# The recurrence's block inverses by Newton steps in four groups over eight PSUM banks, instead of squarings in two halves over four

## The reference

```python
def step(state, inp):
    r_t, w_t, k_t, v_t, kk_t, a_t = inp
    sa = jnp.einsum('bhvk,bhk->bhv', state, -kk_t)
    state = (state * w_t[:, :, None, :]
             + sa[..., :, None] * (kk_t * a_t)[..., None, :]
             + v_t[..., :, None] * k_t[..., None, :])
    out = jnp.einsum('bhvk,bhk->bhv', state, r_t)
    return state, out
...
o = jnp.zeros((B, S, H, N), f32)
for d in range(2):
    o = o + wkv7_scan(rh, heads(decay), kd, vh, kk, heads(a), reverse=(d == 1))
```

## Time and profile before

| | |
|---|---|
| median of three runs | 3305.81 us (3300.61, 3305.81, 3305.88) |
| the profiled execution's own time | 3306.75 us |
| its span, first to last instruction | 3305.0 us |
| TensorE busy | 3113.0 us, 94% of the span |
| VectorE busy | 2296.5 us, 69% |
| ScalarE busy | 975.3 us, 30% |
| GpSimd busy | 1106.5 us, 33% |
| the recurrence stage | 177 to 456.4 us of the span |

### The profile page before, as it was taken

The page is one execution under the profiler, slowest core; times in us unless marked ns, Lnnn a source line. Parts: engine busy times, 40 slices in busy tenths (PEclk is TensorE's granted clock), DMA queues, the critical chain, the costliest instruction groups (busy, mean ns, idle before and its releaser), DMA issues. The chain is left out here.

```text
span 3305.0 us, 57848 instructions
## 1 busy us (share of the span) xinstructions
PE 3113.0 (94%) x21263; PEld 2736.6 (83%) x21263; DVE 2296.5 (69%) x3997; ACT 975.3 (30%) x1689; POOL 1106.5 (33%) x766
## 2 busy tenths in 40 slices
PE   8979979999999999989999999889998999799989
PEld 6568857789999999989999987667886777578867
DVE  7677666779889898778888876576773326567731
ACT  2333431233433433333333332541120013311200
POOL 4231114222222122143333334124554332345543
PEclk9989999999999999999999999999999999899999
DMA  4000012257777877889999943022323220123323
GB/s 159 26 2 3 3 33 96 102 181 245 267 258 240 282 250 254 296 311 369 338 356 337 353 170 105 17 71 87 97 79 87 82 62 29 56 93 100 99 66 96
DMA packets 214343, 509.06 MB, mean 154 GB/s; under 512 B 18534, under 2 KB 102646, under 8 KB 210588
## 3 DMA queue, kind: packets, MB, share of 16 engines
q1 hardware_dynamic: 155420, 322.15, 29.1%
q0 software_dynamic: 36864, 134.23, 12.2%
q10 hardware_dynamic: 21888, 50.34, 4.0%
HBM read 454.21 MB, written 52.44 MB: 153 GB/s over the span
## 5 line engine op out<-in xcount | busy, mean ns | idle before, releaser
L188 PE MATMUL ev_acc<-ev_w_high,ev_high 128*128 128x384 f32 x1024 | 343.2, 335 | 9.3 <-DVE ev_w_low L2569 9.3
L190 PE MATMUL ev_acc<-ev_w_high,ev_low 128*128 128x384 f32 x1024 | 343.0, 335 | 0.0
L189 PE MATMUL ev_acc<-ev_w_low,ev_high 128*128 128x384 f32 x1024 | 343.0, 335 | 0.0
L2519 POOL DMA_INDIRECT ev_rows<-in_v,ev_list x128 | 179.3, 1401 | 328.0 <-DVE ev_row_sum L2574 305.1
L188 PE MATMUL up_ps<-ffn_high,up_high 128*128 128x512 f32 x704 | 276.8, 393 | 5.5 <-DVEq L667 5.5
L190 PE MATMUL up_ps<-ffn_high,up_low 128*128 128x512 f32 x704 | 275.6, 391 | 0.0
L189 PE MATMUL up_ps<-ffn_low,up_high 128*128 128x512 f32 x704 | 275.4, 391 | 0.0
L183 POOL TENSOR_TENSOR up_low<-normed,up_high 128x1024 fp32r<-128x1024 f32 x88 | 211.4, 2403 | 178.0 <-DVE up_high L178 178.0
L188 PE MATMUL eu_ps<-norm_unit_high,eu_high 128*128 128x384 f32 x768 | 265.5, 346 | 0.0
L190 PE MATMUL eu_ps<-norm_unit_high,eu_low 128*128 128x384 f32 x768 | 257.6, 335 | 0.0
L189 PE MATMUL eu_ps<-norm_unit_low,eu_high 128*128 128x384 f32 x768 | 257.3, 335 | 0.0
(11 more groups left out here) (642 smaller groups left out, 8133.4 us busy)
## 6 DMA issues: line engine op xcount, KB each, us to landing
normed<-in_u SPq DMA_DIRECT2D x128, 512.0 KB, 5.1
mixed<-in_v SPq DMA_DIRECT2D x128, 512.0 KB, 5.5
normed<-in_w_up SPq DMA_DIRECT2D x88, 512.0 KB, 3.5
expert_act<-mixed ACTq DMA_DIRECT2D x128, 192.0 KB, 4.2
expert_gates<-eu_gates ACTq DMA_DIRECT2D x24, 1024.0 KB, 6.8
expert_scores<-expert_gates SPq DMA_DIRECT2D x16, 1536.0 KB, 11.6
ev_act<-expert_act SPq DMA_DIRECT2D x128, 192.0 KB, 5.7
in_w_raw<-in_w_in SPq DMA_DIRECT2D x20, 512.0 KB, 3.5
```

Of the source, the lines that this page charges most:

```text
L188: nc.tensor.matmul(out, w_high.bitcast(F32R), x_high.bitcast(F32R), start=start, stop=False)
L189: nc.tensor.matmul(out, w_high.bitcast(F32R), x_low.bitcast(F32R), start=False, stop=False)
L190: return nc.tensor.matmul(out, w_low.bitcast(F32R), x_high.bitcast(F32R), start=False, stop=stop)
L2519: nc.gpsimd.indirect_dma_start(rows[:, b % 4, :], None, v, bass.IndirectOffsetOnAxis(ap=list_[:, b % 8:b % 8 + 1], axis=0)).then_inc(fetch ...
```

## The change

- The inverse X of A = I - L is found by Newton's steps, X becomes 2X - XAX. For each of levels 1 to 5 TensorE forms "E" from X and L - I, ScalarE copies it, TensorE forms "T" from E and X, and VectorE does X = 2X + T in one `scalar_tensor_tensor`. The squarings are gone.
- The eight units go in four groups of two: an E and a T of a group are four products each, a copy or an update is 128x128 elements. E uses banks 3, 4, 5, 1 and T banks 0, 6, 7, 2.
- "Lt" and "L" are formed in blocks of 64: 16 products of 64x64x64 for Lt instead of 8 of 64x128x128, 24 for L instead of 8. VectorE copies each in two pieces of 128x256, with the masks for a 64 block made once ahead of the stage by six small copies. The off-diagonal block of L is copied by ScalarE ("low0", "low1").
- I + L transposed ("Tt") and L - I ("less") are made by GpSimd, after its part of `prepare`.
- The inverse has a tile of its own, and VectorE copies "sa0" ahead of "z_t".

The core of the diff, in this order: tiles and banks, GpSimd, ScalarE, VectorE, TensorE.

```diff
-        inverse_t = c.y[:, 9, :].rearrange("p (u s) -> p u s", s=HEAD)
+        inverse_t = sb("inverse_t", [P, 2 * ST, HEAD])
+        upper, lower, unit = (sb(x, [P, HEAD]) for x in ("block_upper", "block_lower", "block_unit"))
...
-        ab_bank, t_bank = (ps[3], ps[1]), (ps[0], ps[2])
+        e_bank, t_bank = (ps[3], ps[4], ps[5], ps[1]), (ps[0], ps[6], ps[7], ps[2])
+        c_bank, y_bank = (ps[3], ps[1]), (ps[0], ps[2])
+        of_group = lambda i: slice(2 * i, 2 * i + 2)
...
+                def front(d, m):
+                    units_ = unit[:, :].unsqueeze(1).to_broadcast([P, 2 * ST, HEAD])
+                    dve_s[d].wait(pool, m, "Lt1")
...
+                    pool_s[d].ends(nc.gpsimd.tensor_tensor(inverse_t[:, :, :], square[:, :, HEAD:P], units_, ALU.add), "Tt")
+                    dve_s[d].wait(pool, m, "L1")
...
+                    pool_s[d].ends(nc.gpsimd.tensor_tensor(pw[:, :, 0:HEAD], pw[:, :, 0:HEAD], units_, ALU.subtract), "less")
...
+                    if at == 2:
+                        dve_s[d].wait(act, m, "L1")
+                        for h in range(2):
+                            act_s[d].ends(nc.scalar.activation(pw[second_half[d], ST * h:ST * h + ST, HEAD:P], ps[2 + h][second_half[d], :, HEAD:P], ACT.Copy), f"low{h}")
...
+                    for n in range(1, LEVELS):
+                        for i in range(4):
+                            pe_s[d].wait(act, m, f"E{n}{i}")
+                            act_s[d].ends(nc.scalar.activation(square[:, of_group(i), 0:HEAD], e_bank[i][:, 0:2, 0:HEAD], ACT.Copy), f"E{n}{i}")
+                            if i % 2:
+                                beside((n - 1, i // 2))
...
+                    beside((0, 1))
+                    for n in range(1, LEVELS):
+                        for i in range(4):
+                            mine = inverse_t[:, of_group(i), :]
+                            pe_s[d].wait(dve, m, f"T{n}{i}")
+                            done.ends(nc.vector.scalar_tensor_tensor(out=mine, in0=mine, scalar=2.0, in1=t_bank[i][:, 0:2, 0:HEAD], op0=ALU.mult, op1=ALU.add), f"T{n}{i}")
+                            if i % 2:
+                                beside((n, i // 2))
...
-                    pe_s[d].wait(dve, m, "z_t")
-                    done.ends(nc.vector.tensor_copy(z_t[:, :, :], ps[4][:, :, :]), "z_t")
...
                         if n == 0:
+                            done.wait(dve, m, "X1")
                             done.ends(nc.vector.tensor_copy(s_a, u), "sa0")
+                            pe_s[d].wait(dve, m, "z_t")
+                            done.ends(nc.vector.tensor_copy(z_t[:, :, :], ps[4][:, :, :]), "z_t")
...
+                        if kind in ("Lt", "L"):
+                            for x in half:
+                                for h in range(2):
+                                    ins = nc.tensor.matmul(ps[2 * n + h][x, t, 0:HEAD], to_[half[h], x], of_[half[h], x], start=True, stop=True)
+                        if kind == "L":
+                            for h in range(2):
+                                ins = nc.tensor.matmul(ps[2 * n + h][second_half[d], t, HEAD:P], to_[half[h], second_half[d]], of_[half[h], first_half[d]], start=True, stop=True)
...
+                    for n in range(1, LEVELS):
+                        for i in range(4):
+                            if n == 1:
+                                pool_s[d].wait(pe, m, "less")
+                                if i == 3:
+                                    dve_s[d].wait(pe, m, "qk1")
                             else:
+                                dve_s[d].wait(pe, m, f"T{n - 1}{i}")
+                            for k in range(2):
+                                u = 2 * i + k
+                                for x in half:
+                                    ins = nc.tensor.matmul(e_bank[i][x, k, 0:HEAD], inverse_t[x, u, :], pw[x, u, 0:HEAD], start=True, stop=True)
+                            pe_s[d].ends(ins, f"E{n}{i}")
+                        for i in range(4):
+                            act_s[d].wait(pe, m, f"E{n}{i}")
+                            if n == 1 and i == 0:
+                                dve_s[d].wait(pe, m, "qk0")
+                            if n == 1 and i == 3:
+                                act_s[d].wait(pe, m, "U")
+                            for k in range(2):
+                                u = 2 * i + k
+                                for x in half:
+                                    ins = nc.tensor.matmul(t_bank[i][x, k, 0:HEAD], square[x, u, 0:HEAD], inverse_t[x, u, :], start=True, stop=True)
+                            pe_s[d].ends(ins, f"T{n}{i}")
```

More of the change, by code:

```diff
@@ L1265, in _ @@
                         prepare(d, m)
+                        front(d, m)
             @block.scalar
@@ L1331, in _ @@
                     prepare(0, 0, at)
-                for at in ("begin", 0, "end"):
+                for at in ("begin", 0, 2, "end"):
                     front(0, 0, at)
@@ L1371, in prepare @@
                         done.ends(nc.vector.tensor_tensor(f[d][:, here], flat(chunks(gt)[:, here, last]), mid[:, there], ALU.add), "f")
-                def mask_of(d, kind):
-                    first, other, with_self = (c.upper, c.lower, c.upper_eq) if d == 0 else (c.lower, c.upper, c.lower_eq)
-                    return {"Lt": first, "L": other, "zk": first, "qb": with_self, "qk": with_self}[kind]
                 def front(d, m, at):
@@ L1381, in front @@
                     kind, done = kinds[at], dve_s[d]
-                    if kind == "qk":
-                        done.wait(dve, m, "Lt11")
-                        for x in range(2):
-                            unit = c.ident[half[x], half[x]].unsqueeze(1).to_broadcast([HEAD, 2 * ST, HEAD])
-                            done.ends(nc.vector.tensor_tensor(inverse_t[half[x], :, :], square[half[x], :, HEAD:P], unit, ALU.add), f"Tt{x}")
                     pe_s[d].wait(dve, m, kind)
-                    if kind == "Lt":
+                    if kind in ("Lt", "L"):
+                        block = mask_of(d, kind).to_broadcast([P, ST, HEAD])
@@ L1389, in front @@
                         for h in range(2):
-                            for x in range(2):
-                                block = mask_of(d, kind)[half[x], half[x]].unsqueeze(1).to_broadcast([HEAD, ST, HEAD])
-                                done.ends(nc.vector.tensor_tensor(square[half[x], ST * h:ST * h + ST, HEAD:P], ps[h][half[x], :, half[x]], block, ALU.mult), f"Lt{h}{x}")
+                            own = square[:, ST * h:ST * h + ST, HEAD:P] if kind == "Lt" else pw[:, ST * h:ST * h + ST, 0:HEAD]
@@ L1393, in front @@
+                            done.ends(nc.vector.tensor_tensor(own, ps[2 * at + h][:, :, 0:HEAD], block, ALU.mult), f"{kind}{h}")
                         return
                     for h in range(2):
-                        mask = mask_of(d, kind)[:, :].unsqueeze(1).to_broadcast([P, 4, P])
-                        dve_s[d].ends(nc.vector.tensor_tensor(to[d][kind][:, 4 * h:4 * h + 4, :], ps[2 * (at % 2) + h][:, :, :], mask, ALU.mult), f"{kind}{h}")
+                        done.ends(nc.vector.tensor_tensor(to[d][kind][:, ST * h:ST * h + ST, :], ps[2 * (at % 2) + h][:, :, :],
+                                                          mask_of(d, kind).to_broadcast([P, ST, P]), ALU.mult), f"{kind}{h}")
@@ L1398, in solve @@
                 def solve(d, m, beside):
                     done = dve_s[d]
-                    for n in range(LEVELS):
-                        for h in range(2):
-                            if n:
-                                mine = inverse_t[:, ST * h:ST * h + ST, :]
-                                pe_s[d].wait(dve, m, f"T{n}{h}")
-                                done.ends(nc.vector.tensor_tensor(mine, t_bank[h][:, :, 0:HEAD], mine, ALU.add), f"T{n}{h}")
-                            beside((n, h))
+                    beside((0, 1))
@@ L1485, in matrices @@
                         act_s[d].wait(pe, m, "vn")
+                    elif n == 2:
+                        dve_s[d].wait(pe, m, "Lt1")
+                    elif n == 3:
+                        dve_s[d].wait(pe, m, "L1")
+                        act_s[d].wait(pe, m, "low1")
                     else:
-                        dve_s[d].wait(pe, m, last_of[kinds[n - 2]])
+                        dve_s[d].wait(pe, m, "zk1")
                     for t in range(ST):
-                        for h in range(2):
-                            rows = slice(h * HEAD, (h + 1) * HEAD)
-                            ins = nc.tensor.matmul(ps[2 * (n % 2) + h][:, t, :], chunk(left, t)[rows, :], chunk(right, t)[rows, :], start=True, stop=True)
+                        to_, of_ = chunk(left, t), chunk(right, t)
+                        if kind in ("Lt", "L"):
+                            for x in half:
[4 more added lines that the diff above has]
```

(4 more changed lines are left out.)

76 lines of the change are left out of this document (25 added, 51 removed).

## The result

The kernel after the change takes 3270.93 us (median of four runs, 3267.22 to 3274.78), the kernel before it 3303.21 (four runs, 3297.81 to 3305.88): a ratio of 0.9905, with a 95% interval from 0.9893 to 0.9918. That is 32.3 us, between 27.1 and 35.3. Predicted were 3285 us and a gain of 21.

What follows compares the result with a forecast made beforehand. TensorE's weight loads were taken to bound the solves, the state chain and VectorE in turns the steps; 14.9 + 5.95 + 0.5 - 0.36 = 21.0 us off 3306.75, adjusted to the median, gave 3285, range 3275 to 3299 (likeliest case 3277 to 3292).

Steps and rivals of the forecast that it cites:

- What bounds the stage: Recurrence stage, 279.4 us: TensorE bounds the solves; what the stage saves should reach the program's end one for one.
- The undisturbed solve: Solve with nothing beside it: 320 loads, levels of 1.87 us set by TensorE, 9.53 us in all.
- The solve with `prepare`: Solves with `prepare` between: lumps add 2.90 or 2.21 us, giving 12.43 or 11.74; eight solves gain 14.9 us.
- E22: Level 2 of a solve: an E product group starts 1.42 us late (0.73 for direction 0) behind VectorE's differences.
- T32: Level 3 of a solve: a T product group is 0.45 us late behind ScalarE's exponential of 512 columns.
- E50: Start of a solve's level 5: TensorE idles, 0.93 us late, after z and f on VectorE delay level 4's updates.
- The steps: Steps stretches between solves: 0.57 us from sa0's new place, 0.94 in all before E; 5.95 us over seven, 0.5 for the last.
- The start: First front, standing alone: 0.24 us back, mask copies ahead of the first cumulative sum cost 0.6; net 0.36 lost.
- Small copies do not overlap: Rival for the solves: each further 128-wide copy adds 0.284 us, 4.8 in all, 3290; chance with dearer lumps 0.19.
- The update costs 0.42: Rival for the solves: VectorE's update takes 0.42 us, costing 17 us of the 21, time 3302; chance 0.10.
- The waits cost TensorE its pace: Rival for the solves: 0.18 us lost at each of 40 groups, 57.6 us in all, 3342; chance 0.07.
- Better: Rival: lumps fall where a group is late anyway, and a shorter restart (0.05): 3276; chance 0.06.

Runs made afterwards that it cites:

- The kernels with `prepare` spread: Changed kernel with each piece of `prepare` alone at a level's end: 3262.88 us, ratio 0.9867; with the mask copies also later, 3261.74 us.
- The bursts: Changed kernel plus six bursts of 16 unused 64x64x64 products, differing in the array quadrants that follow each other: whole execution 3282.90 us.
- the order over two quadrants: Changed kernel with Lt and L's diagonal blocks formed first on the two diagonal quadrants, then on the other two: 3278.89 us, ratio 0.992.

## Why the prediction was wrong

**What bounds the stage: right.** What was saved in the stage reached the end, 30.0 us by the traces and 32.3 (27.1 to 35.3) by the medians. The two profiled executions differ by 39.5 us (3306.75 and 3267.22), so 9.5 of these lie outside the stage, where the code is the same. The windows view puts 5.7 of them in one place: the same 1001 multiplications took 217.21 us from 2735.22 on before, at a mean granted clock of 0.92, and 211.49 us from 2701.38 on after, at 0.96. So most of it is the clock of these two executions and not the change. The 14 us by which the time lies below the forecast are then the 9.0 of the stage, 2.3 outside it, and 2.6 because the kernel before had a median of 3303.21 us in this set and 3305.81 when the forecast was made.

**The undisturbed solve: right.** 9.53 us predicted, 9.47 measured. A level is 1.87 us: TensorE sets the pace, and the copies come back in time.

**The solve with `prepare`: places right, prices each a little high.** In the first solve E22 1.31 us (predicted 1.42), T32 0.34 (0.45), E50 0.85 (0.93), f's exponential nothing (0.1), the end 0.15 (0.2). The common part is the restart: TensorE loads 0.05 us after the update it waits for (199.53 + 0.48 is the second update's end; the first ends near 199.81, the load is at 199.86), and the 0.11 was read from one row. Four solves at 11.96 for 12.43 and three at 11.25 for 11.74 make 3.3 of the 3.5 us missed here.

One of those prices was right by luck. The 1.92 us of z and f was read as work, though f has three columns. The timeline of the kernel before shows it beside GpSimd:

```profile
207.77 1.59 POOL L1260 TENSOR_TENSOR scan_ek<-mix_kd,scan_ek 128x512 f32<-128x512 f32 x1
...
208.17 1.22 DVE L1371 TENSOR_TENSOR scan_f<-mix_p,scan_mid 128x3 f32<-128x3 f32 x1
```

GpSimd's product ends at 209.36 and f at 209.39. In the kernel after the pair ends alike, 205.90 and 205.93. It was a wait for GpSimd, which no step of the prediction named. The kernels with `prepare` spread show that most of it can be avoided: f takes 0.37 us there on the mean.

**The steps: the step that failed.** The prediction said that L "follows 2.14 later as before", and that L takes "48 loads, 1.39 us for 0.97: 0.42 more on TensorE". Measured, L follows Lt by 1.67 us, and the next load follows L by 1.08 for the 1.48 predicted: 0.87 us a stretch less, which over seven is 6.1 of the 9.0 us by which the stage was missed. The 0.029 us a load was taken from the solve, whose products alternate between two quadrants; Lt and L go round four, at 0.015. The bursts and the order over two quadrants show 0.57 of the 0.87. The other 0.30 stays even over two quadrants. Of it 0.19 is counting: Lt in blocks of 64 was given the time of the wide products it replaced (1.10 us to the next load), though by the prediction's own 0.029 its 32 loads cost 0.93, and over two quadrants they took 0.91. The 0.11 that are left are L's (1.37 for 1.48), and no run takes them apart. All else in this part holds: `kv0` loads 0.44 us after z_t's copy began (predicted 0.44), Lt starts 2.39 after it (2.38), the rest of the stretch is 7.03 (7.0), and "less" hides.

**The start: mis-sized.** Six mask copies were put at 0.6 us between nothing and 1.38. They cost 1.45: the cumulative sum behind them begins 2.30 us after the table load for 0.85. Each is about 0.2 us long, though it has a quarter of the elements of the 0.23 us copy. With them the start lost 1.0 us for 0.36, and the granted clock had a share in it that no run parts: it stood at 0.50 for 14.7 us after the table load for 11.7 before.

**The rivals.** *Small copies do not overlap* did not come: levels are 1.87 us. With it falls the rule of the Trainium skill ("VectorE: DVE Perf Modes", the section on the TRN2 errata) as one that would decide here. It speaks for instructions of 512 elements and more; here updates twice as wide in half as many groups made a level 2.37 us for 1.87 and the stage 12.85 longer. *The update costs 0.42* fell: 284 ns over 160. *The waits cost TensorE its pace* fell: 9.41 us of loads in 9.47 with forty groups. *Better* came nearest, with its short restart of 0.05 right, and at 3276 was still 5 us too slow, since it looked for more in the solves alone and for nothing in the steps.

## What to carry to other kernels

Before a rate per load is carried from one place to another, look at which 64x64 quadrants of the array the successive products use: going round four gave twice the pace of two and four times that of one, for the price of a loop order. That is for 64 columns moving; with 128 the cut into four quadrants brought 0.1 us a stretch. In a loop that lives on a round trip, put side work on the returning engines one piece at a time at a level's end, and keep VectorE's operations on SBUF inputs away from GpSimd's products. A three-column operation of 1.2 us was a wait and not work.

## What the runs showed of the hardware

- fp32 64x64x64 products: 0.058 us a load on one quadrant, 0.029 on any two, 0.015 on four, at the full granted clock, whether or not the quadrants share rows or columns.
- VectorE and GpSimd hold each other up on SBUF. A VectorE operation on two SBUF inputs that began while a GpSimd product ran ended a fixed time after the product, whatever was left of it: 0.55 us after for the difference of 128x512 (1.65 us long for 0.68), 0.02 us after for the 128x3 of f (1.22, 0.30 or 0.18 us long). Copies of 64x64 from SBUF to SBUF did the same, 0.05 us after (two in 1.45 us for 0.41). GpSimd's product went from 1.27 to 1.59 us beside z. The Trainium skill ("GPSIMD Engine Reference", section 1, Specifications) names SBUF interfaces that the two share, with contention for VectorE's instructions with two SBUF inputs: the traces agree, and in them the whole instruction is waited for.
- TensorE's granted clock fell to its 1.2 GHz level in the last steps of two versions, for 3.4 and 6.6 us, and stayed at 1.00 in the kernel after in the same place. These last steps were 1.6 us longer, sa0's old place among it, and 2.3 us longer.
- A fp32 copy of 64x64 from SBUF to SBUF took 0.19 us on VectorE, one of 128x128 0.23.
